# Expert products turned round: gathered rows stationary in fp32r halves, context rows in fp32 on four column groups

## What is computed

```python
def ec_moe(h, p):
    cap = EC_FACTOR * n // N_EXPERTS          # 128 latent rows, 16 context rows per expert
    aff = softmax(xt @ p['router'])
    gate, idx = lax.top_k(aff.T, cap)
    xe = jnp.take(xt, idx, axis=0)
    hid = silu(xe @ w_gate) * (xe @ w_up)     # 1024x1024 matrices, one set per expert, fp32
    ye = (hid @ w_down) * gate[..., None]
    out = zeros.at[idx].add(ye)               # then x = x + g2 * out
```

## Time and profile before

| | |
|---|---|
| median of three runs | 3709.72 us |
| the profiled execution's own time | 3704.16 us |
| its span | 3702.4 us |
| mean granted TensorE clock | 0.938 of 2.4 GHz |
| PE busy | 3307.2 us (89%) |
| PEld busy | 2957.4 us (80%) |
| DVE busy | 1428.2 us (39%) |
| ACT busy | 1245.2 us (34%) |
| POOL busy | 203.8 us (6%) |
| queue of SP | 526.03 MB |
| queue of GpSimd (gather, scatter) | 33.56 MB |

### The profile page before, as it was taken

One profiled execution on the slowest core, in us unless ns is written; L12 is line 12 of the kernel. 1 busy time (PEld: TensorE's weight loads), 2 busy tenths in 40 slices (PEclk: granted clock), 3 DMA queues, 4 the chain that ended last, 5 costly groups with the idle time before them and its releaser, 6 DMA issues. The chain is left out here.

```text
span 3702.4 us, 61080 instructions
## 1 busy us (share of the span) xinstructions
PE 3307.2 (89%) x23418; PEld 2957.4 (80%) x23418; DVE 1428.2 (39%) x2683; ACT 1245.2 (34%) x2772; POOL 203.8 (6%) x175
## 2 busy tenths in 40 slices
PE   6986988996899999998788998889992899999998
PEld 2545777783799999998677787777882899999997
DVE  1466666647000000000676675767747100000000
ACT  2353646621211111111456373654620211111111
POOL 0001000000000000000100101010000000000000
PEclk7997999995899999999898999999995899999998
DMA  8200000138788778884310100100131788887883
GB/s 326 66 14 20 1 4 19 53 114 300 273 283 276 272 271 275 288 272 147 94 38 8 38 1 7 38 7 21 42 114 68 261 279 291 281 276 272 272 279 113
DMA packets 305518, 562.16 MB, mean 152 GB/s; under 512 B 29045, under 2 KB 64570, under 8 KB 305338
## 3 DMA queue, kind: packets, MB, share of 16 engines
q1 hardware_dynamic: 295216, 526.03, 39.8%
q0 software_dynamic: 9216, 33.56, 4.4%
q10 hardware_dynamic: 906, 0.23, 0.0%
HBM read 522.95 MB, written 36.84 MB: 151 GB/s over the span
## 5 line engine op out<-in xcount | busy, mean ns | idle before, releaser
L1879 PE MATMUL psum<-moeh_xe,moe_w 128*128 128x144 f32 x8192 | 1016.6, 287 | 6.0 <-ACT moeh_xe L1915 6.0
L1879 PEld LDWEIGHTS psum<-moeh_xe,moe_w 128*128 128x128 f32 x8192 | 1011.2, 191 | 6.8 <-ACT moeh_xe L1915 6.8
L1895 PE MATMUL psum<-moeh_hid,moe_w 128*128 128x144 f32 x4096 | 531.6, 287 | 1.4 <-DVE moeh_hid L1956 1.4
L1895 PEld LDWEIGHTS psum<-moeh_hid,moe_w 128*128 128x128 f32 x4096 | 514.3, 190 | 6.6 <-issue 4.7
L1956 DVE TENSOR_TENSOR moeh_hid<-moe_act,psum 128x144 f32<-128x144 f32 x256 | 77.8, 304 | 1093.6 <-ACT moe_act L1925 1093.6
L948 PE MATMUL psum<-attn_w_hi,attn_hs 128*128 128x256 f32 (+2 forms) x1440 | 376.4, 346 | 81.8 <-DVE attn_w_lo L1204 71.7
L1925 ACT ACTIVATE moe_act<-psum 128x144 f32<-128x144 f32 x256 | 74.3, 290 | 931.5 <-PE psum L1879 931.5
L948 PEld LDWEIGHTS psum<-attn_w_hi,attn_hs 128*128 128x128 f32 x1440 | 259.2, 194 | 112.5 <-DVE attn_w_lo L1204 73.3
L1290 DVE TENSOR_REDUCE attn_neg_max<-psum 128x1 f32<-128x1280 f32 (+1 forms) x216 | 292.3, 1355 | 99.6 <-PE psum L993 97.8
L993 PE MATMUL psum<-attn_ks,attn_qst 128*128 128x512 f32 (+2 forms) x1200 | 290.3, 377 | 22.4 <-ACT attn_qst L1068 11.6
L1125 ACT ACTIVATE attn_e<-psum,attn_neg_max 128x1280 f32<-128x1280 f32 (+1 forms) x216 | 264.7, 1226 | 73.6 <-DVE attn_neg_max L1290 73.1
(11 more groups left out here) (233 smaller groups left out, 3630.9 us busy)
## 6 DMA issues: line engine op xcount, KB each, us to landing
moe_w<-in_l_w_gate SPq DMA_DIRECT2D x64, 2048.0 KB, 8.7
moe_w<-in_l_w_up SPq DMA_DIRECT2D x64, 2048.0 KB, 13.3
moe_w<-in_l_w_down SPq DMA_DIRECT2D x64, 2048.0 KB, 9.6
ada_w<-in_l_ada_w SPq DMA_DIRECT2D x48, 1024.0 KB, 14.1
out_w<-in_l_w_out SPq DMA_DIRECT2D x16, 512.0 KB, 5.0
h_rows<-mix_xs SPq DMA_DIRECT2D x16, 512.0 KB, 2.6
attnw_w<-in_l_w_in SPq DMA_DIRECT2D x16, 512.0 KB, 6.9
attnw_w<-in_l_w_in SPq DMA_DIRECT2D x6, 1024.0 KB, 8.5
```

What stands on the lines that cost most here:

```text
L1879: last = pe.matmul(m.psum[:, at:at + ROWS], mm.w[2 * (f // 4) + i][:, k, col:col + P], mm.xe[:, k, :], start=(k == 0), stop=(k == KB - 1))
L1895: last = pe.matmul(m.psum[:, at:at + ROWS], mm.w[4 + n // 4][:, f, (n % 4) * P:(n % 4 + 1) * P], mm.hid[:, f, :], start=(f == 0), stop=(f ...
```

## The change

`moe_memory`, `routing` and `experts` are rewritten. A slot is now 1 MB of fp32, `raw[0..11]`: eight for gate and up (128 input features of both), four for down (256 hidden features). For the latent rows each slot is split: ScalarE writes `hi` (fp32r, four buffers), VectorE writes `lo` over the raw values in place. The gathered rows, split in the same way by GpSimd, are stationary, 128 columns; the weights move, 512 columns at a time; three products hi hi, hi lo, lo hi. The result has tokens on partitions, so silu and the product are one operation each per expert, the hidden rows are transposed and split, and the down result needs no transpose: one VectorE operation multiplies it by the gate and by g2, which is spread over the partitions in `routing`. The 16 context rows are a 32-column stationary operand in fp32 on four column groups, which read the raw slots before `lo` overwrites them; their result goes to DRAM as rows and is loaded whole (`y_all`, 1 MB) for `context_result`.

```diff
 def context_result(...):
-    def turn_and_place(pe): ...   # 16 transposes, copies by ACT and DVE, 4 products
+    def load(sp):
+        sp.dma_start(mm.y_all[:, :, :], rows).then_inc(loaded, 16)
+    def place(pe):                # the 4 products alone
     def add(dve):
-            dve.tensor_tensor(out[:, cols], psum, x_ctx[:, cols], ALU.add)
+            dve.tensor_tensor(mm.g2[:, 1, cols], psum, mm.g2[:, 1, cols], ALU.mult)
+            dve.drain()
+            dve.tensor_tensor(out[:, cols], mm.g2[:, 1, cols], x_ctx[:, cols], ALU.add)
 def routing(...):  # sync
             if ada:
                 ada.ahead(sp)
-            for i in range(2):
-                mm.load(sp, i, 0)
+            for k in range(4 if ada else KB):
+                mm.load_gu(sp, k, 0)
             if ada:
                 ada.loads(sp)
+                for k in range(4, KB):
+                    ada.wait_free(sp, k - 4)      # used >= 17 + slot
+                    mm.load_gu(sp, k, 0)
+            for i in range(4):
+                if ada:
+                    ada.wait_free(sp, 4 + i)
+                mm.load_dn(sp, i, 0)
             sp.wait_ge(s["topped"], 2)
             sp.dma_start(dram["pair"][0], ...)    # as before
 def routing(...):  # tensor, scalar
+            for c in range(2):
+                for k in range(KB):
+                    pe.matmul(psum, mod[..].broadcast_to([P, P]), m.ident)      # g2_spread
+            act.copy(mm.g2[:, c, :], psum)                                      # g2_read
 def experts(...):  # tensor
+            def ctx_gu(e, half):
+                for k in range(4 * half, 4 * half + 4):
+                    pe.wait_ge(loaded[k], e * 32 + 32)
+                    for g in range(4):
+                        last = pe.matmul(m.psum[32 * g:32 * g + 32, 6 * BANK:7 * BANK], mm.xc[:, k, :],
+                                         mm.raw[k][:, g // 2, (g % 2) * BANK:(g % 2 + 1) * BANK], ...)
+                last.then_inc(s["ctx_done"], 1)
+            def ctx_dn(e):      # 4 slots x 2 x 4 groups, 256 columns each
+            def lat_gu(e, unit, k):
+                pe.wait_ge(s["lo_ready"], unit + 1)
+                for i, (x, w) in enumerate(((x_hi, w_hi), (x_hi, w_lo), (x_lo, w_hi))):
+                    for j in range(2):
+                        for half in range(2):
+                            last = pe.matmul(m.psum[:, at:at + BANK], x[:, k, :], w[:, j, half * BANK:(half + 1) * BANK], ...)
+                last.then_inc(s["lat_done"], 1)
+            def lat_dn(e, unit, n):     # 12 products as well
+            def body(b, last=False):
+                for k in range(KB):
+                    lat_gu(b + 1, b * UNITS + (8 + k), k)
+                    if k == 1:
+                        turn_hid(b); turn_ctx(b); ctx_gu(b + 1, 1)
+                    if k == 5:
+                        ctx_dn(b)
+                for n in range(4):
+                    lat_dn(b, b * UNITS + (16 + n), n)
+                    if n == 0: turn_x(b + 2)
+                    if n == 1: ctx_gu(b + 2, 0)
 def experts(...):  # scalar, body: steps n, high(n) waits loaded and lat_done of unit n - 4
+                high 3, 4, 5; hid_high(b); silu_ctx(b); read_gu_c(b + 1); high 6, 7, 8, 9; read_yc(b)
+                high 10; silu(b + 1); high 11; read_x(b + 2); high 12, 13, 14
+                act.copy(mm.hi[slot % 4][:, :, :], mm.raw[slot][:, :, :])       # high
 def experts(...):  # vector, body
+                read_y(b - 1); low 2, 3; hid_low(b); hid_ctx(b); low 4, 5, 6, 7; low 8, 9; hid(b + 1)
+                low 10, 11; next_rows(b + 3); low 12, 13
+                dve.wait_ge(s["ctx_done"], quads)                               # in low
+                dve.tensor_tensor(mm.lo[slot], mm.raw[slot], mm.hi[slot % 4].bitcast(F32), ALU.subtract)
 def experts(...):  # gpsimd, body
+                scatter(b - 1); place_ctx(b + 2); split_x(b + 2); gather(b + 3)
+                pool.tensor_copy(hi, mm.x_tmp); pool.drain(); pool.tensor_tensor(lo, mm.x_tmp, hi, ALU.subtract)  # split_x
 def experts(...):  # sync, body
+                wait lat_done, load_gu(k, b + 2) for 8 slots; store_yc(b), 4 stores; wait, load_dn(i, b + 1) for 4
```

More of the change, by code:

```diff
@@ L33 @@
 CAP_L, CAP_C = 2 * LAT // EXP, 2 * CTX // EXP
[L34 removed]
+UNITS = 12
 BANK = 512
@@ L1843, in _, with body @@
-            for e in (EXP - 2, EXP - 1):
-                pool.wait_ge(s["y_read"], 2 * e + 2)
-                scatter()
+            def body(b, first=False, more=2):
+                if not first:
+                    scatter(b - 1)
+                if more >= 1:
+                    wait_value(m, pool, s["ctx_done"], b * 3 + 4)
+                    place_ctx(b + 2)
+                    split_x(b + 2)
+                if more >= 2:
+                    gather(b + 3)
+            pool.memset(mm.xc[:, :, :], 0.0)
@@ new lines, in _ @@
+            pool.memset(mm.hid_c[:, :, :], 0.0).then_inc(s["padded"], 1)
+            pool.drain()
+            place_ctx(0)
+            split_x(0)
+            gather(1)
+            split_x(1)
+            gather(2)
+            pool.wait_ge(s["ctx_done"], 2)
+            place_ctx(1)
+            body(0, first=True)
+            with pool.Fori(1, LAST - 2) as b:
+                body(b)
+            body(LAST - 2, more=1)
+            body(LAST - 1, more=0)
+            for e in (LAST - 1, LAST):
+                scatter(e)
@@ new lines, in _ @@
+            turn_x(0)
+            pe.wait_ge(s["padded"], 1)
+            ctx_gu(0, 0)
+            for k in range(KB):
+                lat_gu(0, k, k)
+                if k == 1:
+                    turn_x(1)
+                    ctx_gu(0, 1)
+                if k == 5:
+                    ctx_gu(1, 0)
+            body(0)
+            with pe.Fori(1, LAST - 1) as b:
+                body(b)
+            body(LAST - 1, last=True)
+            for n in range(4):
+                lat_dn(LAST, UNITS * EXP - 4 + n, n)
@@ new lines, in _ @@
+            next_rows(1)
+            for k in range(4):
+                low(k, k, 1)
+            for k in range(4, 8):
+                low(k, k, 2)
+                if k == 5:
+                    next_rows(2)
+            for k in range(2):
+                low(KB + k, k, 3)
+            hid(0)
+            body(0, first=True)
+            with dve.Fori(1, LAST - 2) as b:
+                body(b)
+            body(LAST - 2, more=False)
+            body(LAST - 1, more=False, last=True)
+            read_y(LAST - 1)
@@ L1992, in finish @@
+            for n in (2, 3):
+                low(UNITS * EXP - 4 + n, n, 3 * EXP)
+            dve.wait_ge(s["scattered"], 16 * LAST)
+            read_y(LAST)
 def finish(nc, m, a, sem, mm, x_ctx_dram):
```

501 lines of the change are left out of this document (319 added, 182 removed).

## The result

The changed kernel takes 3664.1 us (median of 4 runs, 3661.1 to 3664.7), the kernel before, on the same chip, 3710.5 (4 runs, 3707.9 to 3713.4). The ratio is 0.9873, 95% interval 0.9856 to 0.9890: 1.3% faster, by 46 us, where 47.5 were forecast. The span of the profiled execution fell from 3702.4 to 3661.9 us, by 40.5 only, since before's profiled execution (3704.2) stood 6.4 us under this median and after's (3663.7) stood 0.4 under its own.

The account below looks back on a forecast made before the run. TensorE, busy without a gap in the expert stages, was taken as the bound; -77 + 19.5 + 10 + 1 - 2 + 1 = -47.5 from 3709.7 gave 3662 us, own range 3640 to 3700, outer bounds 3625 to 3750.

Parts of the forecast that it names:

- the likeliest case: Whole kernel: the forecast of 3662 us, with TensorE setting the pace in both expert stages; chance 0.57.
- The pace: Expert stages: TensorE's period falls from 48.7 to 46.3 us per expert, saving 77 us over 32 experts.
- sets: Context rows' column-group products in the expert stages: eight gate/up sets 6.9 us, eight down sets 3.4, together 10.3 per expert.
- changes of mode: Expert stages: six changes per expert between full array and column groups, 0.1 us lost each, 0.6 per expert.
- Groups side by side: Context products: four column groups run at the same time, 0.86 us per set at the upper clock level.
- Rival 4: Context products: column groups run in turn, 4650 us, or GpSimd's split exceeds 9 us, 3820; chance 0.06 together with rival 5.
- rival 2: Context column blocks: the clock falls, near 3990 us, or 3745 for a quarter of the blocks; chance 0.08.
- rival 5: Latent products: fp32r with this stationary runs in two passes, 4700 us; chance 0.06 together with Rival 4.
- The splits hidden: Expert stages: ScalarE's and VectorE's weight splits cause no stalls, with 3 us left at low(8) and low(12).
- GpSimd: Expert stages: its split of the gathered rows takes 3 us in all; up to 8.9 us costs nothing.
- Routing: Layer 0 routing: pair stores land behind eight weight slots, moving the selection from 938.6 to 958 us, +19.5 us.
- Heads and tails: Expert stage starts and ends: heads 5 us more per layer, +10, and last read_y +1 for two stages.

Follow-up runs that it names:

- run 6: Changed kernel with VectorE subtracting only two columns per row of a weight block and TensorE taking the high half for the low one: 3638.6 us.
- run 7: Changed kernel with VectorE subtracting in full but TensorE taking the high half in place of the low one: 3644.3 us.
- run 9: Changed kernel with the eight sets of the context down product interleaved with eight products of the next unit: 3733.5 us.
- run 4: Changed kernel with four sets of context products per expert instead of sixteen: 3432.0 us.
- run 2: Changed kernel with four extra VectorE subtractions of 128x512 ahead of low(8) and four ahead of low(12) in every expert: 3692.7 us.
- run 3: Changed kernel with eight extra VectorE subtractions of 128x512 ahead of low(8) and eight ahead of low(12) in every expert: 3953.5 us.
- run 1: Changed kernel with layer 0's pair stores and loads issued ahead of the eight weight loads that wait for adaLN slots: 3645.0 us.
- run 8: Changed kernel with the twelve products reordered, both of the high weight block first and that of the low block last: 3662.3 us.
- run 5: Kernel before the change without its context columns, 128 moving columns instead of 144 in every expert product: 3573.4 us.

## Why the prediction was right

The forecast was 3662 us, the measurement 3664; the likeliest case happened, by its mechanism, in both stages that it named. That the two numbers lie 2 us apart is luck in part. From trace to trace, which is how the sum was built, the change is -40.5 us and not -47.5; the medians differ by 46 because before's profiled execution was a quick one. By its own steps:

- **The pace.** Saved: 77 us forecast, 32 x 2.17 = 69 measured. Two errors went into it. The period before was read 0.3 us too short, since one of the fifteen scatter steps is a short one; and the period after was forecast at 46.3 us and measured at 46.8. The terms of the latter were off in both directions: the products 32.6 against 33.3 (231 ns each and not 227, by the low blocks: runs 6 and 7); transposes 2.6 against 2.2 (0.88 + 0.53 + 0.79); sets 10.3 against 10.3; changes of mode 0.6 against 1.0 (run 9). The mis-sized term with a lesson is the last: I read 0.1 us per change off the overlap of neighbouring records, which sees what is lost at one edge of a change and not that the first product behind it starts slower. The Trainium skill's rule (TensorEngine Tiling (Array Packing), Key Properties), that a change of tiling mode drains TensorE, fits the 0.17 us a time; that still leaves the change a gain.
- **Groups side by side.** 0.86 us per set at the upper clock was taken as half of a pitch at the lower one; run 4 has 0.86. Rival 4 was out, and so were rival 2 (the clock stood at 1.00 throughout) and rival 5 (one record per product).
- **The splits hidden.** 3.2 us of slack at low(8) and low(12) against 3 forecast, and TensorE busy without a gap. Runs 2 and 3 show that it is real and how close the edge is: from 3.2 us on each microsecond costs 32 per place, and in run 3, with TensorE waiting 2.8 and up to 3.5 us, the clock added some 90 us more.
- **GpSimd.** 3.4 us for 3, hidden within the period. The Trainium skill (GPSIMD Engine Reference, Elementwise — side-by-side cycle accounting) gives 4497 ns for an add of 2048 elements; half of that, an estimate, is 2.25 us, and the trace has 2.39 for 1024. The copies are another matter: 0.24 us without VectorE's subtractions, 2.24 with them. The Trainium skill (SBUF — State Buffer, SBUF: two separate sides) calls the pair of ports that the two engines share an exclusive lock, held for a whole instruction while the other blocks; runs 4, 6 and 7 agree, with a copy about as long as one subtraction of 2.29 us. The prediction had the rule in mind for the split alone, and within the period the split was spared, because it falls into a pause of VectorE. At the head of a stage both meet: GpSimd's first split holds up VectorE's first low part (four of them take 10.39 us instead of 9.0), for which TensorE waits, and a long copy costs TensorE 1.2 us more. Everything else stayed under cover.
- **Routing.** +18.5 for +19.5, the selection at 958.01 for 958, and run 1 shows that the order of issue is the whole cause.
- **Heads and tails: too high.** +5.5 us per layer was forecast. A stage is 16 periods and a rest: in layer 0 before 801.9 - 16 x 48.99 = 18.1 us, after 770.7 - 16 x 46.82 = 21.6, so +3.5; in layer 1 the same working gives +2.3. The first latent unit did start 10.9 us into the stage (971.24 to 982.13), near the 11.5 of the forecast, but units ran at the upper clock from the second on, and the end got no longer: from TensorE's last record to the next stage 9.5 us, before 10.7. This error of 5 us offsets most of the 7.6 by which the pace fell short.
- **Outside.** Norm +1.1 for -2. Layer 1's attention and mixer, which the change doesn't touch, differ by 2.4 us between the two profiled executions; that is what one execution against another is good for.

## What to carry to other kernels

When a change moves work from a matrix product's weight loads to its moving side, cost the small remainder too: here it gave back 7.6 of the 9.8 us that the main part gained. Read a period between two events that repeat alike, and leave out the last one. Count changes between full-array and column-group products as 0.17 us each and put column blocks next to one another. And when loads are added to a queue, look for the small store that others wait for and issue it first: one reordering was worth 19 us, 40% of what the whole change brought.

## What the runs showed of the hardware that I had not expected

- While VectorE runs 2.3 us subtractions of two on-chip operands, a GpSimd copy of 128x64 takes 2.24 us instead of 0.24, about the length of one such subtraction, and the issue of an indirect gather 2.88 instead of 1.01 (run 6 against run 7). GpSimd's 1024-column operations, 1.04 and 2.39 us, were equally long in all three kernels; in the changed one they fall into a pause of VectorE. Where GpSimd's subtraction came first, it was VectorE's that got longer, by 1.8 us (run 4).
- A unit of twelve fp32r products takes 2.77 us at the upper clock when four of them have the low half as the moving block, and 2.72 when all have the high half (runs 6 and 7); neither VectorE's work nor another order of the twelve changes that (run 8).
- An fp32 product of 128 moving columns gets little cheaper than one of 144: 112 against 122 ns per record (run 5).
- Around a wait of TensorE of 3.5 us the granted clock went from 1.00 to 0.50 and was back some 6 us after it; around one of 2.8 us, in the same kernel, it stayed at 1.00 in one expert and fell in the next (run 3).
